# Two transformer blocks on one core: rows of 528 and 516 tokens split at a multiple of 16 columns, with the halves back to back across two PSUM banks

## What is computed

```
hn = rmsnorm(h);  h = h + even_mixer(hn)          # sparse attention and retention
h = h + conv_ffn(rmsnorm(h), up, gate, conv, down)
hn = rmsnorm(h);  h = h + odd_mixer(hn)           # stick-breaking attention
h = h + conv_ffn(rmsnorm(h), ...)
x = rmsnorm(h)[:, 16:528]                         # meta tokens dropped
x = x + merge(fox, conv, mlstm, window attention) # second block, 512 tokens
x = x + swiglu_ffn(rms_norm(x))
```

## Time and profile before

| | us |
|---|---|
| median of 3 runs | 2404.89 |
| lowest, highest | 2402.09, 2404.93 |
| profiled execution, first to last instruction | 2403.0 |
| TensorE busy in it | 2362.9 |
| VectorE busy | 1096.6 |
| ScalarE busy | 851.5 |
| GpSimd busy | 918.7 |

### The profile page before, as it was taken

How to read it: one execution, slowest core, us unless ns; L and a number is a source line. 1 busy time by engine, 2 the same in 40 slices (tenths; PEclk the granted TensorE clock), 3 DMA queues, 4 the chain that set the end, 5 groups by cost and what they waited for, 6 DMA issues and landing times.

```text
span 2403.0 us, 37842 instructions
## 1 busy us (share of the span) xinstructions
PE 2362.9 (98%) x15330; PEld 2074.3 (86%) x15330; DVE 1096.6 (46%) x1672; ACT 851.5 (35%) x1314; POOL 918.7 (38%) x382
## 2 busy tenths in 40 slices
PE   7999999999999999999999999999999999999999
PEld 7898889999999999998988888776667888888887
DVE  4884343573442533545644425343474337422222
ACT  4334424432222334454322224443464334322222
POOL 4321224344444442223444444422224545444443
PEclk9999999999999999999999999999999999999999
DMA  4221212222222331111232232321212332322232
GB/s 173 71 71 36 73 60 91 82 94 88 88 88 88 105 106 58 53 52 56 88 105 88 89 104 89 106 71 53 88 53 91 120 105 105 104 88 96 96 105 87
DMA packets 33419, 208.08 MB, mean 87 GB/s; under 512 B 3706, under 2 KB 6420, under 8 KB 9240
## 3 DMA queue, kind: packets, MB, share of 16 engines
q1 hardware_dynamic: 29552, 202.00, 24.6%
q10 hardware_dynamic: 3752, 4.41, 0.6%
HBM read 204.27 MB, written 2.12 MB: 86 GB/s over the span
## 4 chain that ended last, share of the span: by engine, by line
issue 60%; POOL 23%; PE 16%; POOLq 1%; DMA 0%; ACT 0%; DVE 0%; SPq 0%; DVEq 0%; ACTq 0%
POOL wl L2480 23%; PE ps L392 14%; PE ps L345 1%; PE ps L327 1%; POOLq L2479 0%; POOLq L2484 0%; DMA raw<-in_w_all 0%; ACT L430 0%; ACT wh L430 0%; PE ps L488 0%; DVE X L463 0%; SPq L2447 0%; DVEq L463 0%; ACTq L429 0%
## 5 line engine op out<-in xcount | busy, mean ns | idle before, releaser
L2480 POOL TENSOR_TENSOR wl<-raw,wh 128x1024 fp32r<-128x1024 f32 x376 | 918.4, 2447 | 1467.7 <-ACT wh L430 1467.5
L430 ACT ACTIVATE wh<-raw 128x1024 fp32r<-128x1024 f32 x376 | 395.1, 1054 | 751.7 <-PE ps L392 500.8
L392 PE MATMUL ps<-Hh,wl 128*128 128x264 f32 (+2 forms) x1736 | 480.6, 325 | 0.0
L392 PE MATMUL ps<-Hl,wh 128*128 128x264 f32 (+2 forms) x1736 | 480.6, 325 | 0.0
L392 PE MATMUL ps<-Hh,wh 128*128 128x264 f32 (+2 forms) x1736 | 480.5, 325 | 0.0
L392 PEld LDWEIGHTS ps<-Hh,wh 128*128 128x128 f32 x1736 | 291.7, 188 | 28.5 <-issue 0.2
L392 PEld LDWEIGHTS ps<-Hh,wl 128*128 128x128 f32 x1736 | 291.1, 188 | 28.1
L392 PEld LDWEIGHTS ps<-Hl,wh 128*128 128x128 f32 x1736 | 291.1, 188 | 27.2
L345 PE MATMUL ps<-Hh,wh 128*128 128x264 f32 (+1 forms) x1056 | 278.9, 328 | 9.1 <-DVE arena L364 8.1
L345 PE MATMUL ps<-Hh,wl 128*128 128x264 f32 (+1 forms) x1056 | 257.1, 307 | 0.0
L345 PE MATMUL ps<-Hl,wh 128*128 128x264 f32 (+1 forms) x1056 | 256.8, 307 | 0.0
(11 more groups left out here) (252 smaller groups left out, 2812.8 us busy)
## 6 DMA issues: line engine op xcount, KB each, us to landing
raw<-in_w_all SPq DMA_DIRECT2D x188, 1024.0 KB, 4.8
X<-in_xT SPq DMA_DIRECT2D x4, 528.0 KB, 9.6
arena<-scratch ACTq DMA_DIRECT2D x2, 1024.0 KB
arena<-in_extra ACTq DMA_DIRECT2D x2, 528.0 KB
out<-X SPq DMA_DIRECT2D x1, 1024.0 KB, 4.3
out<-X SPq DMA_DIRECT2D x4, 256.0 KB, 2.0
arena<-in_extra ACTq DMA_DIRECT2D x2, 264.0 KB
cst<-in_consts SPq DMA_DIRECT2D x1, 448.0 KB, 11.3
```

The costliest lines, as they stand in the source:

```text
L392: mm = pe.matmul(ps[:, 2 * j + h + bank, 0:c1 - c0], w[:, j, k, :], moving(x, blk, c0, c1), start=(at == 0 and part == 0), stop=(at == len ...
L430: act.activation(wh[:, j], raw[:, j // 2, :, P * (j % 2):P * (j % 2) + P], ACT.Copy).then_inc(hi_split, 1)
L2480: pool.tensor_tensor(wl[:, j], raw[:, j // 2, :, P * (j % 2):P * (j % 2) + P], wh[:, j].bitcast(F32), ALU.subtract).then_inc(split_ready[j ...
```

## The change

The halves of a row of 528 are 256 and 272 columns, those of a row of 516 are 260 and 256 (`LOW`). `Hh` and `Hl` hold a row of 528 as one run from place 0, so that the second half begins at place 256; a row of 516 stands at places 12 to 527, its halves begin at 12 and 272, and the single matmuls of 512 columns at 16. In PSUM the first half is put at the end of its bank and the second at the start of the next, so that a reader sees one run of 528 or 516 columns (`half_acc`, `wide_acc`). `Yh` and `Yl` keep their rows of 528; the halves begin at 0 and 256, or at 12 and 272.

```diff
-HALF = 320
+ROW = 640
+LOW = {528: 256, 516: 260}
...
-        Hh, Hl = sb("Hh", [P, KB, 2 * HALF], F32R), sb("Hl", [P, KB, 2 * HALF], F32R)
+        Hh, Hl = sb("Hh", [P, KB, ROW], F32R), sb("Hl", [P, KB, ROW], F32R)
         def normed(T):
             if T == T1:
-                return [h.rearrange("p b (h n) -> p b h n", h=2)[:, :, :, 0:T1 // 2] for h in (Hh, Hl)]
+                return [h[:, :, 0:T1] for h in (Hh, Hl)]
             if T == T3:
-                return [h[:, :, 0:T3] for h in (Hh, Hl)]
+                return [h[:, :, META - LEAD:T1] for h in (Hh, Hl)]
...
         def halves(T):
-            return [(0, T // 2), (T // 2, T)] if T != T2 else [(0, T2)]
+            return [(0, LOW[T]), (LOW[T], T)] if T != T2 else [(0, T2)]
...
+        def half_acc(bank, h, c0, c1, T, rows=slice(0, P)):
+
+            if T == T2 or (h == 0 and c1 > LOW[T]):
+                return ps[rows, bank + h, 0:c1 - c0]
+            at = 0 if T not in LOW else (512 - LOW[T], -LOW[T])[h]
+            return ps[rows, bank + h, at + c0:at + c1]
+
+        def wide_acc(bank, T=T1, rows=slice(0, P)):
+
+            return ps[rows, bank:bank + 2, :].rearrange("p a b -> p (a b)")[:, 512 - LOW[T]:512 - LOW[T] + T]
+
         def acc(j, T):
-            return ps[:, 2 * j:2 * j + 2, 0:T // 2] if T != T2 else ps[:, 2 * j, :]
+            return wide_acc(2 * j, T) if T != T2 else ps[:, 2 * j, :]
...
                         for h, (c0, c1) in enumerate(spans(T, b)):
-                            mm = pe.matmul(ps[:, 2 * j + h, 0:c1 - c0], w[:, j, k, :], moving(x, k, c0, c1),
+                            mm = pe.matmul(half_acc(2 * j, h, c0, c1, T), w[:, j, k, :], x[:, k, c0:c1],
...
-            o, src, r = cols(dst, T1), ps[:, bank:bank + 2, 0:264], cols(rs_view(T1), T1)
+            o, src, r = dst, wide_acc(bank), rs_view(T1)
...
-                        mm = pe.matmul(ps[:, bank + h, c0 - h0:264], d["V"][0:R, s, 256 * hh + P * b:256 * hh + P * b + P],
-                                       d["AT"][0:R, hh, a:a + h1 - c0], start=(s == 0), stop=(s == (2, 4)[h]),
+                        mm = pe.matmul(half_acc(bank, h, c0, h1, T1), d["V"][0:R, s, 256 * hh + P * b:256 * hh + P * b + P],
+                                       d["AT"][0:R, hh, a:a + h1 - c0], start=(s == 0), stop=(s == (1, 4)[h]),
```

More of the change, by code:

```diff
@@ L344, in three_products @@
                 for h, (c0, c1) in enumerate(halves(T)):
-                    mm = pe.matmul(ps[:, bank + h, 0:c1 - c0], w[:, j, k, :], moving(x_, blk, c0, c1),
+                    mm = pe.matmul(half_acc(bank, h, c0, c1, T), w[:, j, k, :], x_[:, blk, c0:c1],
                                    start=(first and part == 0), stop=(last and part == 2))
@@ L391, in body @@
                                 for h, (c0, c1) in enumerate(spans(T, b)):
-                                    mm = pe.matmul(ps[:, 2 * j + h + bank, 0:c1 - c0], w[:, j, k, :],
-                                                   moving(x, blk, c0, c1), start=(at == 0 and part == 0),
+                                    mm = pe.matmul(half_acc(2 * j + bank, h, c0, c1, T), w[:, j, k, :],
+                                                   x[:, blk, c0:c1], start=(at == 0 and part == 0),
                                                    stop=(at == len(ks) - 1 and part == 2))
@@ L487, in norm_pe @@
             for h, (c0, c1) in enumerate(halves(T)):
-                mm = pe.matmul(ps[:, 2 * j + h, 0:c1 - c0], ones, views[1][:, c0:c1], start=True, stop=True)
+                mm = pe.matmul(half_acc(2 * j, h, c0, c1, T), ones, views[1][:, c0:c1], start=True, stop=True)
             if both:
@@ L507, in norm_act @@
                 x = X[:, b, off:off + T]
-                n_hi.by(act.activation(normed(T)[0][:, b], norm_cols(x, T), ACT.Copy, scale=param(gain, b)))
+                n_hi.by(act.activation(normed(T)[0][:, b], x, ACT.Copy, scale=param(gain, b)))
                 if stage is not None:
@@ L543, in norm_dve @@
                     n_hi.take(v, "dve")
-                    h_ready.by(v.scalar_tensor_tensor(out=xl[:, c], in0=norm_cols(X[:, c, off:off + T], T),
+                    h_ready.by(v.scalar_tensor_tensor(out=xl[:, c], in0=X[:, c, off:off + T],
                                                       scalar=param(gain, c), in1=xh[:, c].bitcast(F32),
@@ L1026, in dsa_pe @@
                     for h, (c0, c1) in enumerate(halves(T1)):
-                        mm = pe.matmul(ps[64:128, 2 + h, 0:264], ident[0:64, 0:64], d["ikk"][0:64, c0:c1], start=True,
+                        mm = pe.matmul(half_acc(2, h, c0, c1, T1, slice(64, 128)), ident[0:64, 0:64], d["ikk"][0:64, c0:c1], start=True,
                                        stop=True)
@@ L1136, in dsa_dve @@
                     sig["idx_dup"].take(v, "dve")
-                    sig["idx_dup_read"].by(v.tensor_copy(cols(d["ikk"][64:128], T1), ps[64:128, 2:4, 0:264]))
+                    sig["idx_dup_read"].by(v.tensor_copy(d["ikk"][64:128], wide_acc(2, T1, slice(64, 128))))
                     turned_all(v, "dve")
@@ L1253, in ret_fill_dve @@
                 v.wait_ge(unit_done[u % 4], u // 4 + 1)
-                x = cols(X[:, b, :], T1)
+                x = X[:, b, :]
                 bank = ret_bank(u)
-                v.tensor_tensor(x, ps[:, bank:bank + 2, 0:264], x, ALU.add).then_inc(acc_free[u % 4], 1)
+                v.tensor_tensor(x, wide_acc(bank), x, ALU.add).then_inc(acc_free[u % 4], 1)
         def rot_pe(pe, d, g, n, bank):
@@ L1260, in rot_pe @@
             for h, (c0, c1) in enumerate(halves(T1)):
-                mm = pe.matmul(ps[:, bank + h, 0:c1 - c0], d["rot"], x[:, c0:c1], start=True, stop=True)
+                mm = pe.matmul(half_acc(bank, h, c0, c1, T1), d["rot"], x[:, c0:c1], start=True, stop=True)
             sig["rot_made"].by(mm)
@@ L1269, in rot_dve @@
             v.wait_ge(sig["rot_made"].sem, 4 * g + n + 1)
-            dve.by(v.tensor_tensor(cols(x, T1), ps[:, bank:bank + 2, 0:264], cols(d["sin"], T1), ALU.mult))
+            dve.by(v.tensor_tensor(x, wide_acc(bank), d["sin"], ALU.mult))
             dve.last(v)
@@ L1308, in ret_var @@
             for h, (c0, c1) in enumerate(halves(T1)):
-                mm = pe.matmul(ps[:, h, 0:264], ones, d["sq"][:, 0, c0:c1], start=True, stop=True)
+                mm = pe.matmul(half_acc(0, h, c0, c1, T1), ones, d["sq"][:, 0, c0:c1], start=True, stop=True)
             sig["ret_var"].by(mm)
@@ L1374, in ret_square @@
             bank = R_OUT + 2 * (i % 2)
-            sig["ret_sq"].by(act.activation(cols(d["sq"][:, i % 2], T1), ps[:, bank:bank + 2, 0:264], ACT.Square))
+            sig["ret_sq"].by(act.activation(d["sq"][:, i % 2], wide_acc(bank), ACT.Square))
         def ret_root(act, d, g, hh):
@@ L1451, in ret_norm @@
                 bank = R_OUT + 2 * b
-                sig["ret_t"].by(v.tensor_tensor(cols(d["t"][:, b], T1), ps[:, bank:bank + 2, 0:264],
-                                                cols(d["sd"], T1), ALU.mult))
+                sig["ret_t"].by(v.tensor_tensor(d["t"][:, b], wide_acc(bank), d["sd"], ALU.mult))
             sig["ret_t"].last(v)
```

31 lines of the change are left out of this document (11 added, 20 removed).

## The result

The changed kernel is slower by a little: a median of 2407.98 us over 18 runs, against 2404.82 for the kernel before, run beside it as often. The ratio is 1.0018, with a 95% interval of 1.0011 to 1.0025. The forecast was 2397.

What follows compares the result with a forecast made beforehand. TensorE, busy 98% of the span, was taken as the bound. Terms 0 + 3.9 + 2.6 - 0.3 + 1.6 gave 7.8 us gained from 2404.9, so 2397 us; range over the cases 2366 to 2405, the forecast's own 2392 to 2402.

Steps and rivals of the forecast that it cites:

- What bounds the kernel: Whole kernel: TensorE, busy 98% of the span at full clock, so nearly each nanosecond on a matmul reaches the end.
- (a): Hh and Hl, rows of 528: 2616 pairs become 256 and 272, a pair stays at 240.0 ns, taken as 0.
- (c): 512-column matmuls in rows of 516: start in column 16, 528 x 5.0 ns, 2.6 us gained.
- (d): Rows of 516, pairs of 258 become 260 and 256: 0.5 us lost from Hh, 0.2 gained from Yh, together 0.3 lost.
- (e): Plain fp32 product L1297: one of 8 matmuls goes in each of 8 calls, 0.2 us each, 1.6 us gained.
- The line between 264 and 512 columns: TensorE's aligned matmul price: straight in width, 0.430 ns a column, so 256 costs 116.6 ns and 272 costs 123.4.
- a lost rhythm: Rival, Hh's matmuls: alternating widths break the even 120.0 ns step, 5232 x 1.3 = 6.8 us back, 2404 us; chance 0.09.
- (b): Yh and Yl, rows of 528: second half begins in column 256, 1632 matmuls at 120.0 for 122.4 ns, 3.9 us gained.
- the 5 ns for a start in column 12: Pairs of 260 and 256: a start off a multiple of 16 columns was taken to cost about 5 ns more.
- (f): VectorE and ScalarE readers of PSUM: one run over two banks in place of two runs costs nothing, taken as 0.
- the price for each started 16 columns: Rival, matmul steps: about 7.06 ns per started group, 256 and 272 cost 233.3 ns a pair, 2369 us; chance 0.27.
- Coarse steps: Rival, matmul steps: price in steps of 13.33 ns, a pair of 256 and 272 costs 253.3 ns, 2442 us; chance 0.09.

Runs made afterwards that it cites:

- the kernel with PSUM alone: Kernel before with only PSUM as in the change (back to back across two banks, read as one run), halves equal, Hh and Hl unchanged: ratio 1.0005.

## Why the prediction was wrong

Its number, its sign and its range failed: a gain of 7.8 us was forecast, and at the second block the changed kernel was 1.95 late. By its steps:

- **What bounds the kernel** was right. A nanosecond on a matmul of a saturated stretch came through, and no wait took the place of one. What it read wrongly is the clock, which is not full in every slice. It falls to 1.2 GHz for short stretches in both kernels, and one such stretch more or less moves a time by 1.6 us or more.
- **(a) Hh's pairs, taken at 0**, is the step that failed most. The steps rose by 3.3 ns in 576 matmuls, by 0.7 in 768, by 2.0 in another 576. These three stretches lost 3.6 us. All of (a) is known only as the rest: at the second block the changed kernel is 1.95 us behind, while (c), (d) and (e) had gained about 4.8 by then (1.4, 1.7 and 1.7), so (a) cost some 7 us. A part lies before 501.9 us, where the two are level though (e) had gained its 1.7. The line between 264 and 512 columns was drawn through two points, 120.0 and 226.7, which are the lowest steps that any run showed for these widths. What moved them was the distance between the halves (3.3 ns alone) and the two widths in turn (1.7 alone), and neither is a term of the line. The prediction saw 120.0 and 121.3 with the same code and gave a lost rhythm 0.09, at a price of 1.3 ns; that rival was the nearest, but it was priced too low, and it called the result no change.
- **(b) Yh, 3.9 us gained.** 122.4 became 121.7 in one stretch, 122.3 became 122.5 in the next and 121.6 became 122.3 in the third. These cancel, and nothing is left of the 3.9 us. Rows 528 places apart took 122.4 or 122.5 in Hh with either split. The term was sized from Yh against Hh as if only the start differed; the distance of the rows differed too, and with that of Yh, Hh took the same 122.4.
- **(c) the 512s, 2.6 us gained.** The step fell from 231.7 to 229.0, 528 x 2.7 = 1.4 us. Place 16 is better than place 4, but not because it is a multiple of 16: place 32 gives 232.1.
- **(d) the pairs of 258, 0.3 us lost.** 119.5 became 118.3 and 120.5 became 119.3, 1.7 us gained over 1440 matmuls. The sign was wrong: the 5 ns for a start in column 12 were added to pairs that turned out cheaper. No cost of the start in column 12 or of PSUM from column 252 on was seen.
- **(e) 1.6 us gained** was right: 8 x 0.21 = 1.7.
- **(f) readers, 0**, was right, as the kernel with PSUM alone shows.

The other 1.6 us between the profiled spans are the clock's, for which the prediction had no term.

Of the rivals, the price for each started 16 columns is refuted: 272 and 256 columns gave 123.3 and not 116.7. Coarse steps are too: no even stretch of Hh came near 126.7. The Trainium skill (TensorE: Matmul & The Clock Gate, section Back-to-back issue gap) gives its gap, straight in N, for an isolated matmul; taken for this stream it was right in that the new split gave no gain. The trace does not agree that N alone sets the step of the stream: 512 columns took 226.7 to 233.3 ns.

What stays open is why. That TensorE's reads of the moving rows meet its reads of the next weights in SBUF would fit the 512s and the shift by 64 bytes, but no run looks at those reads. It fits the 264s badly, which the same shift left alone. For them no rule in places was found that gives 120.0, 121.1, 121.7, 122.4 and 123.3. Nor is it known why one stretch of the kernel before took 121.3 and two others 120.0; the kernel with PSUM alone repeats it. Yh and Yl with rows 640 places apart were not tried; the place of the norm's result in the same tensor stands in the way.

## What to carry to other kernels

Where TensorE is saturated, a change of layout is a change of price: measure the step from start to start before and after, in each stretch, and compare only stretches that differ in one thing. Here equal halves in flat rows (264 and 264, rows 640 places apart) with the 260 and 256 of the short rows are 0.25% faster than the kernel before by the ratio, and 4.5 us or 0.19% by the steps behind 501.9 us. With the short rows at place 124 the steps gain 1.2 us more. A moving operand of 512 columns did best when its start and that of the weights were equal modulo 512 bytes; for two halves in turn the layout has to be tried.

Where an effect is a few tenths of a per cent, look at the granted clock in windows of a few us first. Short stretches at half clock come and go between executions, and the tenths on the page don't show them.

## What the runs showed of the hardware that was not expected

- A matmul of 128 x 128 weights with 512 fp32r columns steps at 226.7, 229.0, 231.7, 232.1 or 233.3 ns. Its row begins 0, 64, 16 or 128 bytes beyond the weights modulo 512, or 64 bytes short of them, in this order. A period of 256 bytes instead of 512 is not excluded.
- The step of 264 columns went from 120.0 to 123.3 ns with distance between halves and rows; with equal halves, their place in PSUM had no effect on it, nor had a shift of the weights by 64 bytes.
- A start off a multiple of 16 columns costs nothing by itself: place 264 gave 120.0.
- The woven part of the second block takes 547.1, 548.7 or 551.9 us in kernels that do not differ there. The profiled runs differ in how much of it has the low clock: 0.91, 0.83 and 0.91 from 1575 to 1595 us, 0.94, 0.94 and 0.77 from 1645 to 1675.
